# Hybrid encoder block on one core: products with V packed into two passes of 128 columns, sums of exponentials on GpSimd

## The reference

```python
def one_block(qblk):
    s = jnp.einsum('bqhd,bkhd->bhqk', qblk, k).astype(jnp.float32) * scale
    p = jax.nn.softmax(s, axis=-1).astype(v.dtype)
    return jnp.einsum('bhqk,bkhd->bqhd', p, v)
```

## Time and profile before

| | |
|---|---|
| runs shown | 1372.26, 1372.17, 1361.59 us; median 1372.17 |
| profiled execution | 1364.26 us, span 1362.5 us |
| mean granted PE clock | 0.98 |
| PE busy | 1307.2 us (96%), 6218 products |
| DVE busy | 957.7 us (70%) |
| ACT busy | 629.7 us (46%) |
| POOL busy | 128.3 us (9%), 101 instructions |
| DMA | 64.27 MB, mean 47 GB/s |

### The profile page before, as it was taken

The page is one execution under the profiler, slowest core; times in us unless marked ns, Lnnn a source line. Parts: engine busy times, 40 slices in busy tenths (PEclk is TensorE's granted clock), DMA queues, the critical chain, the costliest instruction groups (busy, mean ns, idle before and its releaser), DMA issues.

```text
span 1362.5 us, 17828 instructions
## 1 busy us (share of the span) xinstructions
PE 1307.2 (96%) x6218; PEld 1046.7 (77%) x6218; DVE 957.7 (70%) x1459; ACT 629.7 (46%) x959; POOL 128.3 (9%) x101
## 2 busy tenths in 40 slices
PE   5999998799999999999799999999999999999998
PEld 5999997466666667687578888888888888888886
DVE  5687659777777775576868766667777766667755
ACT  6486825377776775533444242433324242433320
POOL 0000033300000001322001010110101010110101
PEclk9999899699999999999799999999999999999999
DMA  6011200000000014200022112121112022121103
GB/s 210 32 51 39 70 0 1 1 1 9 9 9 10 9 56 148 84 10 25 0 57 75 33 62 67 38 69 31 62 31 69 28 64 69 38 69 32 62 31 124
DMA packets 30569, 64.27 MB, mean 47 GB/s; under 512 B 6483, under 2 KB 7187, under 8 KB 30517
## 3 DMA queue, kind: packets, MB, share of 16 engines
q1 hardware_dynamic: 30516, 63.57, 14.6%
HBM read 59.20 MB, written 4.23 MB: 47 GB/s over the span
## 4 chain that ended last, share of the span: by engine, by line
PE 48%; DVE 1%; issue 1%; ACT 0%; DVEq 0%
PE banks L2495 30%; PE banks L100 6%; PE banks L101 6%; PE banks L102 6%; DVE halo_acc L2332 0%; PE banks L2502 0%; DVE slot_l L2267 0%; ACT gate_conv L2196 0%; DVE up_raw L2288 0%; DVE up_raw L2283 0%; DVE gate L2339 0%; ACT slot_h L2125 0%; DVE halo_acc L2329 0%; DVE up_first L2339 0%; DVE gate_conv L2347 0%
## 5 line engine op out<-in xcount | busy, mean ns | idle before, releaser
L2495 PE MATMUL banks<-x_hi,slot_h 128*128 128x512 f32 x616 | 245.4, 398 | 2.3 <-DVE slot_l L2267 1.3
L2495 PE MATMUL banks<-x_hi,slot_l 128*128 128x512 f32 x616 | 244.0, 396 | 0.0
L2495 PE MATMUL banks<-x_lo,slot_h 128*128 128x512 f32 x616 | 243.9, 396 | 0.0
L2267 DVE TENSOR_TENSOR slot_l<-up_raw,slot_h 128x512 fp32r<-128x512 f32 x131 | 103.8, 793 | 151.9 <-ACT slot_h L2125 151.1
L2125 ACT ACTIVATE slot_h<-up_raw 128x512 fp32r<-128x512 f32 x131 | 82.2, 627 | 173.4 <-PE banks L2495 171.1
L2495 PEld LDWEIGHTS banks<-x_hi,slot_h 128*128 128x128 f32 x616 | 116.2, 189 | 34.1 <-DVE gate L2339 2.8
L100 PE MATMUL banks<-dn_h,a_h 128*128 128x512 f32 x352 | 137.9, 392 | 2.6 <-issue 2.6
L101 PE MATMUL banks<-dn_l,a_h 128*128 128x512 f32 x352 | 137.6, 391 | 0.0
L102 PE MATMUL banks<-dn_h,a_l 128*128 128x512 f32 x352 | 137.4, 390 | 0.0
L2495 PEld LDWEIGHTS banks<-x_hi,slot_l 128*128 128x128 f32 x616 | 116.2, 189 | 27.0
L2495 PEld LDWEIGHTS banks<-x_lo,slot_h 128*128 128x128 f32 x616 | 116.3, 189 | 26.5
(11 more groups left out here) (302 smaller groups left out, 2552.8 us busy)
## 6 DMA issues: line engine op xcount, KB each, us to landing
up_raw<-in_w_up SPq DMA_DIRECT2D x88, 256.0 KB, 2.7
dn_raw<-in_w_down SPq DMA_DIRECT2D x22, 512.0 KB, 4.2
win_raw<-in_w_in SPq DMA_DIRECT2D x11, 512.0 KB, 3.3
x_tm<-in_x_tm SPq DMA_DIRECT2D x8, 512.0 KB, 4.3
wo_raw<-in_w_out SPq DMA_DIRECT2D x16, 256.0 KB, 4.1
h<-in_x_tm SPq DMA_DIRECT2D x8, 512.0 KB, 5.6
out<-h SPq DMA_DIRECT2D x16, 256.0 KB, 2.0
sum_recip<-recip SPq DMA_DIRECT2D x8, 256.0 KB, 3.5
```

The costliest lines, as they stand in the source:

```text
L2267: nc.vector.tensor_tensor(s_l[slot], x, f32(s_h[slot]), ALU.subtract).then_inc(sem["up_lo"], 1)
L2495: ins = nc.tensor.matmul(o, s[slot][:, k], xs[w], start=fresh and k == 0 and n == 0, stop=k == 3 and n == 2, skip_group_check=not fresh)
```

## The change

For the first six heads (`PACKED`) the columns of ones are left out of `pv`. Low and high parts of V are taken side by side as 128 columns, once by `e_h` and once by `e_l`: two products a tile and chunk. `o_ps` then holds the low part's result in partitions 0 to 63 and the high part's in 64 to 127. The low part is now also multiplied by `e_l`.

The two halves are added up after ACT's copy: SP moves the upper half of `o_sb` into `sum_recip` (`fold_in`), and GpSimd adds it to the lower half (`fold`). The sums of the exponentials are added up by GpSimd from `e_f`, tile by tile (`add_e`), into `e_sum`; at the head's end it splits the total into a high and a low part, which take the buffers of `e_h` and `e_l` that the meta tile leaves free. Two new side jobs of the next head, `s0` and `s1` (step 1, last two places), sum over the partitions with three products each against ones, the meta tile's share among them, and DVE copies the results into `s_row`. `recip_row` starts from there. `ys` moves by one step. New waits: ACT's `e_f` on the addition of the tile three before, DVE's low half of tile 1 and ACT's `e_f` of tile 2 on `s1`, the wide row's transfer on the fold.

```diff
--- before.py
+++ after.py
@@ -1030,15 +1030,18 @@
     FIRST = dict(PREPARE)
     FIRST.update({4: ("a5", "", "a6", "a7"), 5: ("a8", "", "a9", "a10"), 6: ("a11", "", "a12", "a13"), 8: ("x0", "x1", "x2", "")})
     META_QUERIES = {5: ("xt", "", "", ""), 7: ("", "", "", "xo")}
-    LRU_SUMS = {1: ("ys", "", "", "")}
+    LRU_SUMS = {2: ("", "ys", "", "")}
+    E_SUMS = {1: ("", "", "s0", "s1")}
+    PACKED = HEADS - 2
     END = HEADS - 1
     NONE = ("", "", "", "")
 
     def side_jobs(h, s):
 
         places = [None] * 4
-        for plan, head in [(FIRST if h < 0 else PREPARE, h + 1), (META_QUERIES, h), (LRU_SUMS, h)]:
-            if 0 <= head < HEADS and not (plan is META_QUERIES and h != END) and not (plan is LRU_SUMS and h != END - 2):
+        for plan, head in [(FIRST if h < 0 else PREPARE, h + 1), (META_QUERIES, h), (LRU_SUMS, h), (E_SUMS, h)]:
+            if 0 <= head < HEADS and not (plan is META_QUERIES and h != END) and not (plan is LRU_SUMS and h != END - 2)\
+                    and not (plan is E_SUMS and not 1 <= h <= PACKED):
                 for i, kind in enumerate(plan.get(s, NONE)):
                     if kind:
                         assert places[i] is None
@@ -1094,6 +1097,24 @@
 
         return ym[half_of(h), h // 2, 0:SEQ]
 
+    e_sum = place("e_sum", M_Z + 1032 + 3 * (D // 2), (SEQ,))
+    s_row = place("s_row", M_ATT + 3 * T, (T,))[QK:QK + 1, 0:SEQ]
+    E_EVENTS = []
+    for h in range(PACKED):
+        E_EVENTS += [("add", h, 1), ("add", h, 2), ("add", h, 3)] + ([("fold", h - 1, 0)] if h else [])
+        E_EVENTS += [("add", h, 4), ("add", h, 5), ("add", h, 6), ("add", h, 7), ("high", h, 0), ("low", h, 0)]
+    E_EVENTS.append(("fold", PACKED - 1, 0))
+
+    def e_count(kind, h, s=0):
+
+        return E_EVENTS.index((kind, h, s)) + 1
+
+    def total_h(h):
+        return e_h[(SLOTS * h + XT) % 3]
+
+    def total_l(h):
+        return e_l[(SLOTS * h + XT) % 2]
+
     def rows(g):
         return P if g % SLOTS < XT else META
 
@@ -1102,11 +1123,20 @@
     def recip_row(eng, h):
 
         eng.wait_ge(sem["o_read"], h + 1)
-        eng.dma_start(rs, o_sb[VD:VD + 1].rearrange("p (a b) -> p a b", b=XT)).then_inc(sem["sums_in"], 16)
+        if h < PACKED:
+            if h:
+                eng.wait_ge(sem["y_mul"], h)
+            eng.dma_start(rb, o_sb[VD:2 * VD]).then_inc(sem["fold_in"], 16)
+            wait_read(eng, ("s1", h + 1))
+            eng.dma_start(rs, s_row.rearrange("p (a b) -> p a b", b=XT)).then_inc(sem["sums_in"], 16)
+        else:
+            eng.dma_start(rs, o_sb[VD:VD + 1].rearrange("p (a b) -> p a b", b=XT)).then_inc(sem["sums_in"], 16)
         eng.wait_ge(sem["sums_recip"], h + 1)
         eng.dma_start(dram["recip"].rearrange("(a b) -> a b", b=XT), rs).then_inc(sem["recip_row"], 16)
         eng.wait_ge(sem["recip_row"], 16 * (h + 1))
-        if h:
+        if h < PACKED:
+            eng.wait_ge(sem["e_sum"], e_count("fold", h))
+        elif h:
             eng.wait_ge(sem["y_mul"], h)
         eng.dma_start(rb, dram["recip"].unsqueeze(0).broadcast_to([VD, SEQ])).then_inc(sem["recip_in"], 16)
 
@@ -1312,6 +1342,32 @@
         settle(nc.gpsimd.tensor_copy(v_m[32:32 + META], vt[:, :, VD:VW]))
         settle(nc.gpsimd.tensor_copy(v_m[64:64 + META, :, 0:VD], vt[:, :, 0:VD]))
 
+        def add_e(h, s):
+            g = SLOTS * h + s
+            pool.wait_ge(sem["e_hi"], g + 1)
+            if s > 1:
+                pool.wait_ge(sem["e_sum"], e_count("add", h, s - 1))
+            elif h:
+                pool.wait_ge(sem["e_sum"], e_count("low", h - 1))
+            nc.gpsimd.tensor_tensor(e_sum, e_f[(g - 1) % 3] if s == 1 else e_sum, e_f[g % 3], ALU.add).then_inc(sem["e_sum"], 1)
+
+        def fold(h):
+            pool.wait_ge(sem["fold_in"], 16 * (h + 1))
+            nc.gpsimd.tensor_tensor(o_sb[0:VD], o_sb[0:VD], rb, ALU.add).then_inc(sem["e_sum"], 1)
+
+        for h in range(PACKED):
+            for s in range(1, XT):
+                add_e(h, s)
+                if s == 3 and h:
+                    fold(h - 1)
+            pool.wait_ge(sem["pv_done"], SLOTS * h + 6)
+            pool.wait_ge(sem["e_sum"], e_count("add", h, XT - 1))
+            nc.gpsimd.tensor_copy(total_h(h), e_sum).then_inc(sem["e_sum"], 1)
+            pool.wait_ge(sem["pv_done"], SLOTS * h + 7)
+            pool.wait_ge(sem["e_sum"], e_count("high", h))
+            nc.gpsimd.tensor_tensor(total_l(h), e_sum, f32(total_h(h)), ALU.subtract).then_inc(sem["e_sum"], 1)
+
+        fold(PACKED - 1)
         for kind, j in ORDER:
             pieces = y_pieces(kind, j)
             for m, (y, high, low_part) in enumerate(pieces):
@@ -1405,6 +1461,7 @@
             if h == END - 1 and s >= 5:
                 split_w(s - 5)
             if (h, s) == (END, 1):
+                act.wait_ge(sem["e_sum"], e_count("low", PACKED - 1))
                 split_y("L", 0)
             if (h, s) == (END, 2):
                 act.wait_ge(sem["wo_lo"], 4)
@@ -1422,7 +1479,8 @@
                 act.wait_ge(sem["pv_done"], SLOTS * h)
                 if h >= 2:
                     act.wait_ge(sem["y_mul"], h - 1)
-                nc.scalar.activation(o_sb[0:VD + 2], o_ps[0:VD + 2], ACT.Copy).then_inc(sem["o_read"], 1)
+                m = 2 * VD if h <= PACKED else VD + 2
+                nc.scalar.activation(o_sb[0:m], o_ps[0:m], ACT.Copy).then_inc(sem["o_read"], 1)
                 if h == HEADS - 1:
 
                     act.wait_ge(sem["x_max"], 1)
@@ -1438,6 +1496,11 @@
                 if g >= 3:
                     act.wait_ge(sem["e_lo"], lows(g - 3))
                     act.wait_ge(sem["pv_done"], g - 2)
+                    h3, s3 = divmod(g - 3, SLOTS)
+                    if h3 < PACKED and s3 < XT:
+                        act.wait_ge(sem["e_sum"], e_count("add", h3, max(s3, 1)))
+                    if h3 < PACKED and s3 == XT:
+                        act.wait_ge(sem["side_done"], number[("s1", h)] + 1)
                 nc.scalar.activation(e_f[g % 3][0:n], s_ps(g)[0:n], ACT.Exp, scale=SCALE)
                 if s == XT:
                     if h == 0:
@@ -1607,6 +1670,11 @@
                 ins = nc.vector.tensor_reduce(mx_all, mx3.rearrange("p (c t) -> p t c", c=3), AX.X, ALU.max)
             elif kind == "ys":
                 ins = var_y(0, side)
+            elif kind in ("s0", "s1"):
+                if h > 1 and kind == "s0":
+                    dve.wait_ge(sem["sums_in"], 16 * (h - 1))
+                c = int(kind[1])
+                ins = nc.vector.tensor_copy(s_row[:, 512 * c:512 * c + 512], side[0:1])
             elif kind == "xt":
                 xe = x_e.rearrange("p t h c -> p (t h) c")
                 ins = nc.vector.tensor_tensor(xe[:, :, 2:4], side[:, 0:NT * NX].rearrange("p (n c) -> p n c", c=2),
@@ -1647,6 +1715,8 @@
                 dve.wait_ge(sem["e_hi"], g)
                 if g - 1 >= 2:
                     dve.wait_ge(sem["pv_done"], g - 2)
+                if 1 <= h <= PACKED and s == 2:
+                    dve.wait_ge(sem["side_done"], number[("s1", h)] + 1)
                 low_half(0)
             for j in js[1:3]:
                 if j:
@@ -1796,6 +1866,15 @@
                 c, t = divmod(int(kind[1:]), XT)
                 ins = nc.tensor.matmul(side, q_h[b][0:QK, tile_of(t)], k_h[b][0:QK, 512 * c:512 * c + 512],
                                        start=True, stop=True)
+            elif kind in ("s0", "s1"):
+                m = h - 1
+                cs = slice(512 * int(kind[1]), 512 * int(kind[1]) + 512)
+                pe.wait_ge(sem["e_sum"], e_count("low", m))
+                pe.wait_ge(sem["e_lo"], lows(SLOTS * m + XT))
+                one = v[:, 0, 2 * VD:VW]
+                nc.tensor.matmul(side[0:2], one, total_h(m)[:, cs], start=True, stop=False)
+                nc.tensor.matmul(side[0:2], one, total_l(m)[:, cs], start=False, stop=False)
+                ins = nc.tensor.matmul(side[0:2], v_m[:, m, VD:VD + 2], e_m[:, cs], start=False, stop=True)
             elif kind == "ys":
                 pe.wait_ge(sem["ysum"], 3)
                 ins = sums_y(0, side)
@@ -1896,7 +1975,14 @@
             cs = slice(512 * c, 512 * c + 512)
             if s == XT:
                 pe.wait_ge(sem["e_lo"], lows(g))
-                ins = nc.tensor.matmul(o_ps[0:VD + 2, cs], v_m[:, h, :], e_m[:, cs], start=False, stop=True)
+                m = VD if h < PACKED else VD + 2
+                ins = nc.tensor.matmul(o_ps[0:m, cs], v_m[:, h, 0:m], e_m[:, cs], start=False, stop=True,
+                                       skip_group_check=h < PACKED)
+            elif h < PACKED:
+                both = v[:, s, at:at + 2 * VD]
+                nc.tensor.matmul(o_ps[:, cs], both, e_h[g % 3][:, cs], start=s == 0, stop=False)
+                pe.wait_ge(sem["e_lo"], lows(g) - 1 + c)
+                ins = nc.tensor.matmul(o_ps[:, cs], both, e_l[g % 2][:, cs], start=False, stop=s == XT - 1)
             else:
```

(2 more changed lines are left out.)

## The result

| | before | after |
|---|---|---|
| median, lowest and highest of four runs | 1371.83 us (1361.59 to 1372.26) | 1434.88 us (1426.01 to 1436.03) |
| ratio | | 1.0486, 95% interval 1.0448 to 1.0525 |
| profiled execution, span | 1364.26, 1362.5 us | 1434.86, 1432.8 us |
| mean granted PE clock | 0.98 | 0.949 |

The account below looks back on a forecast made before the run. PE bounded a head before (34.84 us); after, DVE would: 27.2 + 1.2 copies + 14.9 stopped, less 1.5, is 41.8 us. Six heads add 42 to 1364.3: 1406 us, own range 1379 to 1425, 8 in 10 from 1366 to 1432.

Parts of the forecast that it names:

- The stop of DVE: Attention heads: GpSimd instructions stop DVE instructions with two SBUF inputs until they end; 14.9 us a head.
- About 1.5 falls in waits that stay: DVE, each head: of 43.3 us needed, about 1.5 overlaps remaining waits such as that for `q_h`, leaving 41.8 us.
- the head follows DVE: Six packed heads: PE waits on DVE, so a head takes DVE's 41.8 us instead of 34.84; +42 us.
- rival 3: PE in the heads: clock also falls to half speed behind a 3 us hole; 1416, up to 1440 us; chance 0.13.
- Rival 1: Heads: PE's saving comes through, GpSimd's stops costing DVE under 4.5 us a head; 1344 us; chance 0.13.
- 20 where the stall is filled: PE, six heads: fewer products gain 20 us where `s0` and `s1` fill the wait for `o_sb`.
- Rival 2: Heads: GpSimd starts just behind the second `e_l`, loss 1.0 to 1.15 us each; 1364 to 1374 us; chance 0.14.

Follow-up runs that it names:

- e3: The changed kernel with each GpSimd addition replaced by memsets of about the same total length, which only write: 1362.64 us, ratio 0.998 to the kernel before.
- e1: The changed kernel without GpSimd's additions, fold, copy and subtraction in the heads; packed products stay: 1356.12 us, ratio 0.994 to the kernel before.
- e11: The changed kernel without two of ACT's three exponentials of the meta tile, ahead of `q_h`: 1430.79 us, ratio 1.049 to the kernel before.
- e2: The kernel before, plus only GpSimd's seven additions a head, their result unused: 1426.03 us, ratio 1.044.
- e8: The changed kernel with each GpSimd addition held back until DVE has written both halves of its tile's `e_l`: 1429.30 us, ratio 1.045 to before.
- e14: The changed kernel with each GpSimd addition cut into two instructions of 512 columns: 1392.68 us, ratio 1.022 to the kernel before.
- e5: The changed kernel with each GpSimd addition cut into four instructions of 256 columns: 1398.03 us, ratio 1.023 to the kernel before.
- e9: The changed kernel with DVE's 16 reductions a head over 256 instead of 512 columns: 1412.51 us, ratio 1.035 to the kernel before.
- e4: The changed kernel plus 24 zero-weight products a head, ahead of three side jobs where PE stands still: 1427.69 us, ratio 1.046 to before.
- e13: The changed kernel plus 12 zero-weight products a head, ahead of three side jobs where PE stands still: 1421.32 us, ratio 1.042 to before.

## Why the prediction was right or wrong

**GpSimd's instructions.** Right: 2.39 us for the additions and the subtraction, 22.8 forecast against 23.2 us a head. The copy took 1.04 at its shortest, 1.27 in the median (1.2 taken). The fold took 2.82 in the median, a head's first addition 2.62 (2.40 taken for both).

**The stop of DVE.** Right in kind (e3 shows that reading is what does it) and, in the middle heads, in size: 14.9 us forecast, 13.4 to 13.7 measured. In stretches 1, 2 and 6 it is 10.2, 11.2 and 9.0. `s_row` is busy for 0.683 us each, the upper bound named.

**The step that failed** is the last one of the sum: "About 1.5 falls in waits that stay", so DVE busy 41.8 us a head, and "the head follows DVE". It put DVE's idle time at nothing: of 7.6 us a head, all was to be filled by stopped time and copies. What the runs showed in its place is that none of it was. DVE's busy time in the middle heads came to 41.75 to 42.03, as forecast, but 4.5 to 5.3 us of idle time stood beside it, as much as in the same heads of e1, where nothing stops DVE (4.8 to 5.0). By the waits of the head shown 3.2 us of the 4.45 are for `q_h`, 0.8 for PE's `a` products, 0.2 for `k_h`. In the same head of before they were 2.8, 2.8 and 1.0: only the waits for the `a` products and `k_h` gave way, and those had fallen to 1.4 and 0.2 in e1 already. The prediction saw the 2.60 us wait for `q_h` and booked it as cover; it kept its length. ACT's `q_h` needs transposes that stand behind other products in PE's queue (e11), so when DVE's late work makes PE late, `q_h` comes late as well. That link is read from the timelines; what is measured is that the idle time stayed.

The same sum over six stretches, by what DVE's busy time and the head's length grew:

| run, against | DVE stopped | heads longer |
|---|---|---|
| after, e1 | 70.9 | 72.7 |
| e2, before | 55.6 | 64.2 |
| e8, e1 | 56.1 | 60.3 |
| e14, e1 | 45.0 | 29.9 |
| e5, e1 | 30.4 | 29.6 |
| e3, e1 | 5.0 | 3.5 |

Only with halves did idle time take up a large part of the stops. In e5 and e8 waits for GpSimd itself are in the second number.

**The forecast came nearer than its rule.** It took 27.2 us of own work and 13.4 net of stops for each of six heads, which is too much for three of them. Had every head been as long as DVE's measured busy time, six would have taken 233.0 us, 24 more than before and not 42. The other 41 us are DVE's idle time. That a DVE counted too busy in the first two stretches and the sixth and an idle time left out partly cancel is luck. e9 shows the same from the other side: 4.0 us less DVE work, 2.7 us less head.

**The clock (rival 3, chance 0.13)** was the case, in both of its numbers short: two falls a head, not one, and mostly 6.8 to 10.2 us each, not 3.4. The prediction placed the hole at the last tile, behind add 7, copy and subtract; the one shown is in the tiles before it (393.05 to 395.08), behind a stopped `e_l`. Its upper value of 1440 us, for two falls a head, lies near the measured time, but e4 and e13 show that the clock is not what fills the gap: 61 to 68 us less time at half speed brought back 3 to 14 us. How DVE's idle time divides between the loop and the slower clock isn't settled: with the clock up, 10 to 13 of the 41 us went away, but the added products act on the loop too.

**Rival 1** could not have come through in full even without any stop: 1344 us forecast, 1356 measured (e1). The term of the sum that was too large is "20 where the stall is filled": it gave 8 us, since `s0` and `s1` fill the `o_sb` stall but bring waits of their own for DVE, 0.95 us a head. In the head shown PE's busy time fell by 1.4 us (33.14 to 31.78), against 2.3 forecast; why it is not more isn't shown.

**Rival 2**, the stops packed tightly, was not the case: the additions' median is 2.39 us, as undisturbed, and DVE bears the stops.

**What would be seen.** `r_row` 42 us apart for heads 0 to 5 and about 34 after: 42.8 to 47.3 and 38.0, wrong by that step. DVE busy near 40 a head: 41.8 to 42.0 in three, 32.0 to 38.1 in the others. Mean `e_l` over 1 us with maxima near 3: 1.216 and 2.897, right. Hardly a DVE wait for the `a` products: 18.8 us fell to 13.1, in 17 instead of 28; a quarter gone, not all. New waits of PE for `lam_t`: right, 25.5 us in 20; for `e_l` only one, of 0.4 us. SP and the wide row: no wait of DVE or PE for a transfer appears, as costed; only GpSimd's last fold waits for its own (9.7 us, once).

## What to carry to other kernels

Moving elementwise work to GpSimd isn't free where DVE has instructions with two SBUF inputs: price it per GpSimd instruction that reads SBUF, and count how often it meets one; short instructions cut the price, work that only writes has none. When an added cost makes an engine the bound, don't take its busy time as the new period of the loop: ask of each of its waits whether what ends it comes late too when the engine is late. Here the added time came on top of the old period, nearly whole. And take the engine's work head by head, not from one stretch. Before work is moved off PE, ask what PE's stalls are waiting for: a stall's length is not saved by fewer products.

## What the runs showed that was not expected

- GpSimd's addition by size: 128x256 in 0.75 us (0.72 at the shortest), 128x512 in 1.27 to 1.53, 128x1024 in 2.39. Memset of 1024: 0.955.
- The stopped DVE instruction can be passed over once more: 4.57 us for one that needs 0.68 (e4).
- Holes of about 2 us in PE, with PE busy four fifths of the head (38.74 of 46.3), went with falls to half speed of mostly 6.8 to 10.2 us; about two such a head.
- A transfer that accumulates 512 KB from SBUF to SBUF lands in 4.5 us. Chained on the same target, and issued by GpSimd, one takes 5.5 us.
